# A transformer-layer kernel: one residual tile for all stages, and other places for splits and loads at its changes of stage

## Chip, core and metric

The kernel runs on one core of one Trainium2 chip. The metric is the device time of one launch in microseconds (us), as the median of several runs; less is better.

## What is computed

One decoder layer in float32, for 2048 tokens of width 1024. Cut to what matters here:

```
h = x
# 1. mixer: HGRN2 (4 heads, chunks of 64) beside sliding-window attention (8 heads of 64)
hn = rms_norm(h, norm1_g);  proj = hn @ w_in
h = h + concat(hgrn2(proj), window_attention(proj)) @ w_out
# 2. cross attention to 256 memory tokens, 4 heads of 128
h = h + cross_attention(rms_norm(h, norm2_g), rms_norm(mem, mem_norm_g)) @ xa_wo
# 3. MLP, 1024 -> 4096 -> 1024
a = relu(rms_norm(h, norm3_g) @ mlp_up);  h = h + (a * a) @ mlp_down
```

## The kernel before

All of it is one program in raw engine streams: TensorE (PE), VectorE (DVE), ScalarE (ACT), GpSimd (POOL) and SyncE (SP, the queue of nearly all loads and stores) each run a list written out by hand, and wait for one another on semaphores. The tokens are four blocks of 512, held transposed: a block is a tile of 128 partitions x 8 x 512. A weight panel is 128 x 1024 (512 KB). There are two slots for panels (`raw`, `whi`, `wlo`, index 0 and 1, taken in turn).

**Every product is made in three parts.** A float32 value is held as a high part (`hi`, `whi`: ACT's copy into fp32r) and a low part (`lo` by DVE, `wlo` by POOL: the value less its high part). A product of a panel with a block adds high x high, high x low and low x high: 24 matmuls of 512 columns for a panel of eight 128x128 pieces. So before PE can use a panel, it has been loaded by SP, split by ACT (`whi`, about 1 us) and by POOL (`wlo`, four pieces), and the slot that it goes into has been used up. `take` (ACT or DVE) empties the PSUM bank of a product; PE may start product n once product n-2 is taken.

**The stages**, in the order in which they run:

- `prepare` (L489 on): rope angles, normed memory, memory keys and values, and the norm of the first block. At its end SP stores the angles, the keys and the values to HBM (L566 to L571); the semaphore `kept` counts these three stores to 48.
- `mixer` (L745 on): first the list `FIRST_STEPS`, the products of five panels (numbers 17 to 21: hg_f, hg_q, hg_v, hg_g, sw_k) for the first block, with the gate work of its first head beside them; then four turns, one for each block, by `MIX_STEPS` (the last by `LAST_STEPS`, L238 to L251, made from `MIX_STEPS` by leaving out what prepares a next block). ACT begins with `act.wait_ge(sh["kept"], 48)` ahead of `FIRST_STEPS` (L1225). DVE waits for `kept` too, clears five buffers and sets one (L1278 to L1281), and only then starts its list. The mixed block goes from `yT` to HBM (`mixed_scratch`) in four stores.
- In the last turn, `cross_panel` splits the first panel of the next stage, and `cross_make` 0 to 2 puts its product among the steps of the last attention.
- `cross` (L1691 on): two turns, each for a pair of blocks, in the order `CROSS_WORK` (built at L267 to L333): the products `out` (8 panels for each block), `xq` (4), the attention, `xo` (4 panels with two products each). Products of `out` and `xo` are added to the residual `h` by DVE (L2011). At the end of turn 1 stand the products 32 to 39 (`xo` of the second block), and among them `norm_write`/`norm_store` (the first block of the pair, normed for the MLP, to HBM), `split` 0 to 7 (the high and low part of the first block of the MLP, L1911 and L1999) and `norm_square` 3 0 to 7 (squares of the other block, ACT L1940, summed by DVE L2021 to L2028).
- `mlp` (L2258 on): two halves of two blocks; up products with pairs of panels, the first pairs (`PLAIN`) plain and the others by Strassen's seven products, then 112 steps down. A plain pair makes four products, named by panel and block: "11", "12", "21", "22".

**SP at the change from mixer to cross** (L989 to L1003, L1819 to L1852). After the two stores of `yT`, SP waits for all four stores of the last block. Then it issues, in this order: memory keys and values (512 KB each), the residual block (2 MB, L1830), the second mixed block (2 MB, L1833), cross panel 2, and then each panel i once slot i - 2 is split (L1849 to L1851). The panels 0 and 1 were loaded in the last mixer turn. ACT splits panel 1 only when its mixer list is at its end: `split_panel` is the first step of `CROSS_WORK` (L1919).

**The change from cross to mlp.** SP loads MLP panel 0 into slot 0 as cross panel 32 (split by L1919 and L464), waits for the norm of the pair's first block (L1857), loads the second normed block into `h[:, 0]` (2 MB, L1858), and then MLP panel 1 (L1861). PE waits for the whole split of panel 0 and for all eight low parts of the block (`first_block_split`) before its first MLP product. ACT waits for the last product and the last sum of squares, and then runs `panel(0, 1)`, `moving` B12 and B22 (high parts of the second block), `plain` 11 (takes a product) and so on. DVE makes the low parts and the Strassen sums T1, T3, T2, T4. PE makes the products in the order 11, 12, 21, 22.

**Tiles.** `mixer` holds `yT`, `kq`, `key` and `keep` (the span factors of a head) as tiles of its own, `prepare` its `mT`, `msq`, `mn`; `h` (two blocks, 32 KB a partition) exists only from `cross` on.

Of the kernel before, what the change touches and what calls it, by code (L numbers as in the profile page):

```python
# [266 lines left out]
def cross_steps():  # L267
# [52 lines left out]
    for u in range(HEADS):  # L320
# [118 lines left out]
def layer(nc, xT, memT, pos, con_d, vec_d, sinks_d, w_mix, w_cross, w_mk, w_mv, w_mlp, outT):  # L439
# [6 lines left out]
    with ExitStack() as ctx:  # L446
        def sb(name, shape, dt=F32):
            return ctx.enter_context(nc.sbuf_tensor(name, shape, dt))

        sh = dict(con=sb("con", [P, CON_W]), vec=sb("vec", [P, VEC_W]), eps=sb("eps", [P, 1]), hT=sb("hT", [P, KT, TB]),  # L450
# [4 lines left out]
                  w_hi=ctx.enter_context(nc.semaphore("panel_hi_ready")),  # L455
                  cross_product=ctx.enter_context(nc.semaphore("c_product_ready")),
# [22 lines left out]
        with ExitStack() as inner:  # L479
# [3 lines left out]
            sh |= dict(h=sb("h", [P, 2, KT, TB]), aout=sb("aout", [P, 2, TB]), upper=inner.enter_context(ExitStack()))  # L483
# [5 lines left out]
def prepare(nc, block, sems, sh, memT, pos, con_d, vec_d, sinks_d, w_mk, w_mv, rope_d, mem_d, xT, w_mix):  # L489
# [9 lines left out]
    with ExitStack() as ctx:  # L499
# [13 lines left out]
        mT = sb("mT", [P, KT, MEM])  # L513
        msq = sb("msq", [P, KT, MEM])
        mn = sb("mn", [P, KT, MEM])
# [40 lines left out]
        def _(sp):  # L556
            sp.dma_start(mT[:], memT).then_inc(s_mem, 16)
# [187 lines left out]
def mixer(nc, block, sems, sh, xT, w_mix, rope_d, y_d, w_cross):  # L745
# [17 lines left out]
    with ExitStack() as ctx:  # L763
# [14 lines left out]
        yT = sb("yT", [P, KT, TB])  # L778
# [17 lines left out]
        key = sb("key", [P, TB])  # L796
        keep = sb("keep", [P, TB])
# [7 lines left out]
        kq = sb("kq", [P, NS, TB])  # L805
# [156 lines left out]
        def _(sp):  # L962
# [8 lines left out]
            def turn(blk, last):  # L971
# [20 lines left out]
                sp.dma_start(out[:, HEADS:KT - 1, :], yT[:, HEADS:KT - 1, :]).then_inc(stored[1].sem, 16)  # L992

# [35 lines left out]
        def _(act):  # L1029
# [80 lines left out]
            def turn(blk, steps):  # L1110
                for step in steps:
# [112 lines left out]

            act.wait_ge(sh["kept"], 48)  # L1225
            turn(-1, FIRST_STEPS[1:])
# [464 lines left out]
def cross(nc, block, sems, sh, xT, w_cross, mem_d, y_d, h2_d, normed_d, w_mlp):  # L1691
# [16 lines left out]
    with ExitStack() as ctx:  # L1708
# [34 lines left out]
        h_in = [signal(f"c_residual_loaded_{b}", 1, 16) for b in range(2)]  # L1743

        h_out = [signal(f"c_residual_stored_{b}", 1 + b, 16) for b in range(2)]
        raw_in = [signal(f"c_panel_loaded_{i}", CROSS_PAN // 2, 16) for i in range(2)]
        w_hi = signal("c_panel_hi_ready", CROSS_PAN)
# [68 lines left out]
        def _(sp):  # L1816
# [6 lines left out]
            for turn in range(TURNS):  # L1823
                last = turn == TURNS - 1
                for i in range(1, CROSS_PAN + 1):
                    if i == 1:
# [3 lines left out]
                        sp.dma_start(h[:, 0, :, :], xT[turn * 2]).then_inc(h_in[0].sem, 16)  # L1830
                    if i == 2:
# [16 lines left out]
                    if (turn, i) != (0, 1):  # L1848
# [30 lines left out]
        def _(act):  # L1879
# [33 lines left out]
            for turn, step in CROSS_WORK:  # L1913
                kind = step[0]
                if kind == "split_panel":
# [4 lines left out]
                elif kind == "take" and CROSS_PRODUCTS[step[1]][1] == "xq":  # L1920
# [11 lines left out]
                    act.activation(hsq[:, u % 2, :], PROJ[n % 2][:], ACT.Square).then_inc(q_in.sem, 1)  # L1932
                elif kind == "split":
# [255 lines left out]

def product_order(half):  # L2190


    for n in range(PAIRS):
        yield from ((n, j) for j in (OUTPUTS if n < PLAIN[half] else ("P1", "P2", "P5", "P6", "P3", "P7", "P4")))
# [63 lines left out]
def mlp(nc, block, sems, sh, w_mlp, h2_d, normed_d, hidden_d, outT):  # L2258
# [8 lines left out]
    with ExitStack() as ctx:  # L2267
# [3 lines left out]
        def sem(name):  # L2271
            return sems.enter_context(nc.semaphore(name))
# [128 lines left out]
        w_hi = Tally(sem("m_weight_hi_ready"), w_keys + steps)  # L2401
# [858 lines left out]
```

## Time and profile before

| | us |
|---|---|
| median of 3 runs | 2741.36 (2741.07 to 2743.33) |
| the profiled execution: its own time | 2745.06 |
| its span in the trace | 2743.3 |
| PE busy | 2643.8 (96%) |
| DVE / ACT / POOL busy | 1771.7 / 1146.9 / 1073.5 |

The span is what the trace covers, from the first to the last instruction; the execution's own time is 1.8 us longer. Times in the rows further down are from the span's start, the mean duration of one instruction in ns. PEclk is the clock that was granted to TensorE, as a share of 2.4 GHz: 1.00, or 0.50 for 1.2 GHz. A matmul that follows another starts before that one's end, so the rate of a stretch is read from starts, not from durations. By these times `prepare` ends at about 53, `mixer` at about 1019 and `cross` at about 1499 us.

### The profile page before, as it was taken

The numbers are of one execution on the slowest core, as the hardware profiler recorded it, in microseconds if no ns is written. First come the engines' busy times: TensorE is split into PE (matmuls) and PEld (weight loads), VectorE is DVE, ScalarE is ACT, GpSimd is POOL, SyncE is SP. The second block draws the span as 40 slices with busy tenths as digits, with TensorE's granted clock in tenths as the row PEclk, the third lists the DMA queues.
The fourth block names the chain that finished last, engine by engine and source line by source line (L and its number), as shares of the span: only waits on it lengthen the run. The fifth ranks groups of instructions, "written<-read, shape, count | busy, mean of one in ns | idle before, by whom it ended". The sixth has DMA issues, their size and how long they took to land.

```text
span 2743.3 us, 39704 instructions
## 1 busy us (share of the span) xinstructions
PE 2643.8 (96%) x13654; PEld 2165.0 (79%) x13654; DVE 1771.7 (65%) x3010; ACT 1146.9 (42%) x2179; POOL 1073.5 (39%) x1258
## 2 busy tenths in 40 slices
PE   7999999999999988998998999999999999999999
PEld 5778778777877876786886788878888888888887
DVE  6677567767756754656657587687666354556665
ACT  4455454545544443554465432243223223322332
POOL 1332322233232215525634477647667222222223
PEclk9999999999999989999999999999999999999999
DMA  4211311221131114317314234433334963445664
GB/s 177 95 49 46 110 55 47 69 96 54 40 118 54 45 67 174 107 54 285 130 49 170 85 131 140 160 104 112 123 109 138 314 188 112 134 134 144 202 186 149
DMA packets 172701, 326.17 MB, mean 119 GB/s; under 512 B 11856, under 2 KB 77776, under 8 KB 169808
## 3 DMA queue, kind: packets, MB, share of 16 engines
q1 hardware_dynamic: 167344, 314.08, 34.3%
q10 hardware_dynamic: 5152, 9.51, 0.9%
q8 instruction: 110, 1.80, 0.3%
q14 instruction: 95, 0.78, 0.1%
HBM read 255.26 MB, written 68.29 MB: 118 GB/s over the span
## 4 chain that ended last, share of the span: by engine, by line
PE 80%; DVE 9%; ACT 5%; issue 3%; DMA 2%; POOL 1%; ACTq 0%; DVEq 0%; SPq 0%; POOLq 0%
PE bank L3176 7%; PE bank L3174 7%; PE bank L3178 7%; PE bank L3154 7%; PE bank L3150 6%; PE bank L3151 6%; PE bank L1520 5%; PE bank L1513 5%; PE bank L1516 5%; PE bank L1592 3%; PE bank L2123 3%; PE bank L2118 3%; PE bank L2119 3%; PE bank L1675 2%; PE bank L1652 2%
## 5 line engine op out<-in xcount | busy, mean ns | idle before, releaser
L464 POOL TENSOR_TENSOR wlo<-raw,whi 128x256 fp32r<-128x256 f32 x612 | 506.5, 858 | 992.3 <-ACT whi L1117 648.2
L1513 PE MATMUL bank<-hi,whi 128*128 128x512 f32 x704 | 296.3, 421 | 5.3 <-ACT whi L1117 5.3
L1516 PE MATMUL bank<-lo,whi 128*128 128x512 f32 x704 | 278.8, 396 | 5.9 <-DVE lo L1267 5.9
L3178 PE MATMUL bank<-hi,wlo 128*128 128x512 f32 x896 | 275.8, 389 | 0.0
L3174 PE MATMUL bank<-hi,whi 128*128 128x512 f32 x896 | 275.8, 389 | 0.0
L3176 PE MATMUL bank<-lo,whi 128*128 128x512 f32 x896 | 275.8, 389 | 0.0
L2675 POOL TENSOR_TENSOR wlo<-h,whi 128x256 fp32r<-128x256 f32 x160 | 127.9, 823 | 300.1 <-ACT whi L2736 300.1
L2981 DVE TENSOR_TENSOR lo<-h,hi 128x1024 fp32r<-128x1024 f32 x80 | 124.5, 1557 | 172.8 <-ACT hi L2744 172.8
L2118 PE MATMUL bank<-hi,whi 128*128 128x512 f32 x504 | 210.3, 417 | 24.4 <-ACT whi L1919 17.2
L2119 PE MATMUL bank<-lo,whi 128*128 128x512 f32 x504 | 199.5, 396 | 0.0
L2657 POOL TENSOR_TENSOR wlo<-raw,whi 128x256 fp32r<-128x256 f32 x166 | 150.1, 930 | 121.2 <-ACT whi L2685 118.9
L3178 PEld LDWEIGHTS bank<-hi,wlo 128*128 128x128 f32 x896 | 168.2, 188 | 34.9
L3174 PEld LDWEIGHTS bank<-hi,whi 128*128 128x128 f32 x896 | 168.2, 188 | 34.9
L3176 PEld LDWEIGHTS bank<-lo,whi 128*128 128x128 f32 x896 | 168.2, 188 | 34.9
L1520 PE MATMUL bank<-hi,wlo 128*128 128x512 f32 x704 | 190.3, 412 | 0.0
L2736 ACT ACTIVATE whi<-h 128x512 fp32r<-128x512 f32 x80 | 50.6, 632 | 289.1 <-PE bank L3178 271.3
L1516 PEld LDWEIGHTS bank<-lo,whi 128*128 128x128 f32 x704 | 134.1, 190 | 38.1 <-DVE lo L1267 8.5
L1513 PEld LDWEIGHTS bank<-hi,whi 128*128 128x128 f32 x704 | 134.0, 190 | 37.8 <-issue 10.5
L2657 POOL TENSOR_TENSOR m_xlo<-raw,m_xhi 128x256 fp32r<-128x256 f32 x174 | 162.7, 967 | 0.0
L1520 PEld LDWEIGHTS bank<-hi,wlo 128*128 128x128 f32 x704 | 130.6, 189 | 35.2 <-issue 9.2
L2685 ACT ACTIVATE whi<-raw 128x512 fp32r<-128x512 f32 x87 | 54.5, 629 | 225.0 <-DMA raw<-w_mlp 181.9
L3150 PE MATMUL bank<-hi,whi 128*128 128x512 f32 x348 | 136.1, 391 | 1.7 <-issue 1.7
(387 smaller groups left out, 5981.9 us busy)
## 6 DMA issues: line engine op xcount, KB each, us to landing
h<-hidden_scratch SPq DMA_DIRECT2D x96, 512.0 KB, 4.2
raw<-w_mix SPq DMA_DIRECT2D x88, 512.0 KB, 3.3
raw<-w_cross SPq DMA_DIRECT2D x64, 512.0 KB, 3.3
raw<-w_mlp SPq DMA_DIRECT2D x64, 512.0 KB, 4.7
hidden_scratch<-hT SPq DMA_DIRECT2D x116, 256.0 KB, 2.1
h<-w_mlp SPq DMA_DIRECT2D x112, 256.0 KB, 3.0
hT<-xT SPq DMA_DIRECT2D x4, 2048.0 KB, 9.4
hT<-mixed_scratch SPq DMA_DIRECT2D x4, 2048.0 KB, 8.6
```

Source lines behind the costliest of these rows:

```text
L464: last = pool.tensor_tensor(wlo[:, i, cols], raw[:, i, cols], whi[:, i, cols].bitcast(F32), ALU.subtract)
L1513: pe.matmul(out, w, hi[:, k, :], start=k == 0, stop=False)
L1516: pe.matmul(out, w, lo[:, k, :], start=False, stop=False)
L1520: last = pe.matmul(out, wlo[:, i % 2, k * P:(k + 1) * P], hi[:, k, :], start=False, stop=k == KT - 1)
L2118: pe.matmul(out, w, hi[b][:, k, :], start=k == 0, stop=False)
L2119: pe.matmul(out, w, lo[b][:, k, :], start=False, stop=False)
L2657: last = pool.tensor_tensor(lo_tile[:, cols], source(half, n, w)[:, cols], hi_tile[:, cols].bitcast(F32), ALU.subtract)
L3150: pe.matmul(acc, hi_tile[:, cols], parts(half, m, k)[0], start=k == 0, stop=False)
L3154: last = pe.matmul(acc, lo_tile[:, k * P:(k + 1) * P], parts(half, m, k)[0], start=False, stop=k == KH - 1)
L3174: pe.matmul(down_bank(i)[:], wh[:, cols], xh[:, i % 2, :], start=K == 0, stop=False)
L3176: pe.matmul(down_bank(i)[:], wh[:, cols], xl[:, i % 2, :], start=False, stop=False)
L3178: last = pe.matmul(down_bank(i)[:], wl[:, cols], xh[:, i % 2, :], start=False, stop=K == KD - 1)
```

## The change

It touches the three changes of stage, and what has to hold for that.

- **One tile.** `h` is made once for all stages. `yT` is its second half. `kq`, `key` and `keep` of the mixer lie in its first half, and so do (with four pieces of the second half) `mT`, `msq` and `mn` of `prepare`.
- **prepare to mixer.** ACT does the steps of `FIRST_STEPS` ahead of the first `take` (that is, the split of panel 18) before it waits for `kept`.
- **mixer to cross.** In the last turn SP loads cross panel 2 once panel 0 is split, and the residual block once the last head's scores are made, both ahead of its wait for the last stores. ACT splits cross panel 1 in the last attention (`cross_second`, ahead of `("pv", 12)`). In `cross`, SP no longer loads these, and issues the second mixed block ahead of panel 4, not of panel 2.
- **cross to mlp.** `norm_square` 3 4 to 3 7 move behind all splits; ahead of them ACT splits MLP panel 1 (`mlp_panel`). SP loads MLP panel 1 before the second normed block. PE waits for the high parts alone before its first MLP product, makes high x high and low x high first, and waits for the low parts one by one (`first_plain`). The first pair's order becomes 11, 21, 12, 22, on PE and in the takes and stores; ACT's list at the start of the MLP changes with it.

```diff
@@ LAST_STEPS, CROSS_WORK
-                      (("cross_make", 1), ("scores", _first + 3)), (("cross_make", 2), ("pv", _first))):
+                      (("cross_make", 1), ("scores", _first + 3)), (("cross_make", 2), ("pv", _first)), (("cross_second",), ("pv", _first))):
...
+def last_squares_end(work):
+    end = SEQ // TB // 2 - 1
+    late = [(end, ("norm_square", 3, k)) for k in range(KT // 2, KT)]
+    return [s for s in work if s not in late] + [(end, ("mlp_panel",))] + late
...
+CROSS_WORK = last_squares_end(CROSS_WORK)
@@ prepare, mixer: tiles
-        mT = sb("mT", [P, KT, MEM])
...
+        places = sh["h"][:].rearrange("p i k t -> p (i k) t")
+        mT, msq, mn = (places[:, n * KT // 2:(n + 1) * KT // 2, :].rearrange("p k (a t) -> p (k a) t", t=MEM) for n in range(3))
...
-        yT = sb("yT", [P, KT, TB])
+        residual, yT = sh["h"][:, 0], sh["h"][:, 1]
+        kq, key, keep = residual[:, 0:NS, :], residual[:, NS, :], residual[:, NS + 1, :]
@@ mixer, SP, end of turn
+                if last:
+                    sp.wait_ge(set_up, COUNTS_SET)
+                    wait_all(sp, sh["split_for_cross"])
+                    sp.dma_start(raw[:, 0, :], w_cross[CROSS_SOURCE[2]]).then_inc(sh["cross_raw_in"], 16)
+                    sp.wait_ge(h_sc.sem, h_sc.at(blk, HEADS * NCH // 2 - 1))
+                    sp.dma_start(residual, xT[0]).then_inc(sh["residual_in"], 16)
@@ mixer, ACT
+                    elif kind == "cross_second":
+                        act.wait_ge(set_up, COUNTS_SET)
+                        act.wait_ge(*sh["loaded_for_cross"])
+                        act.activation(whi[:, 1, :], raw[:, 1, :], ACT.Copy).then_inc(sh["cross_hi"], 1)
...
+            first_take = next(n for n, s in enumerate(FIRST_STEPS) if s[0] == "take")
+            turn(-1, FIRST_STEPS[1:first_take])
             act.wait_ge(sh["kept"], 48)
-            turn(-1, FIRST_STEPS[1:])
+            turn(-1, FIRST_STEPS[first_take:])
@@ cross, SP
-                        sp.dma_start(h[:, 0, :, :], xT[turn * 2]).then_inc(h_in[0].sem, 16)
-                    if i == 2:
+                        if turn:
+                            sp.dma_start(h[:, 0, :, :], xT[turn * 2]).then_inc(h_in[0].sem, 16)
+                    if i == (2 if turn else 4):
                         sp.wait_ge(y_lo.sem, y_lo.at(turn, KT - 1))
                         sp.dma_start(y[:], y_d[turn * 2 + 1]).then_inc(y_in[1].sem, 16)
...
-                    if (turn, i) != (0, 1):
+                    if turn or i > 2:
...
+            sp.wait_ge(w_hi.sem, w_hi.at(TURNS - 1, CROSS_PAN - 1))
+            sp.wait_ge(w_lo.sem, w_lo.at(TURNS - 1, CROSS_PAN - 1))
+            sp.dma_start(raw[:, 1, :], w_mlp[1]).then_inc(sh["panel_in"], 16)
             sp.wait_ge(h_out[0].sem, h_out[0].at(TURNS - 1, 0))
             sp.wait_ge(n_w[0].sem, n_w[0].at(TURNS - 1, KT - 1))
             sp.dma_start(h[:, 0, :, :], normed_d[1].rearrange("k p t -> p k t")).then_inc(sh["second_in"], 16)
-            sp.wait_ge(w_hi.sem, w_hi.at(TURNS - 1, CROSS_PAN - 1))
-            sp.wait_ge(w_lo.sem, w_lo.at(TURNS - 1, CROSS_PAN - 1))
-            sp.dma_start(raw[:, 1, :], w_mlp[1]).then_inc(sh["panel_in"], 16)
@@ cross, ACT
-                if kind == "split_panel":
+                if kind == "split_panel" and (turn, step[1]) == (0, 1):
+                    continue
+                elif kind == "split_panel":
...
+                elif kind == "mlp_panel":
+                    act.wait_ge(sh["panel_in"], 16)
+                    act.wait_ge(product.sem, product.at(turn, len(CROSS_PRODUCTS) - 1))
+                    act.activation(whi[:, 1, :], raw[:, 1, :], ACT.Copy).then_inc(sh["mlp_hi"], 1)
@@ mlp, order, ACT, PE
+def plain_order(half, n):
+    return ("11", "21", "12", "22") if (half, n) == (0, 0) else OUTPUTS
...
-            wait_all(act, sh["last_products"] + sh["squares_added"] + sh["norms_stored"])
+            wait_all(act, sh["squares_added"] + sh["norms_stored"])
...
-                    panel(0, 1)
                     moving(0, "B12")
+                    plain(0, 0, "11")
                     moving(0, "B22")
-                    plain(0, 0, "11")
                     moving(0, "T1")
+                    plain(0, 0, "21")
                     plain(0, 0, "12")
+                    panel(0, 2)
                     moving(0, "T2")
-                    plain(0, 0, "21")
-                    panel(0, 2)
                     moving(0, "T4")
...
+            def first_plain(acc):
+                for k in range(KT):
+                    pe.matmul(acc, whi[:, 0, k * P:(k + 1) * P], sh["hi"][:, k, :], start=k == 0, stop=False)
+                for k in range(KT):
+                    pe.matmul(acc, wlo[:, 0, k * P:(k + 1) * P], sh["hi"][:, k, :], start=False, stop=False)
+                y_lo, count = sh["first_block_split"][1]
+                for k in range(KT):
+                    pe.wait_ge(y_lo, count - (KT - 1) + k)
+                    last = pe.matmul(acc, whi[:, 0, k * P:(k + 1) * P], sh["lo"][:, k, :], start=False, stop=k == KT - 1)
+                last.then_inc(made.sem, 1)
...
-            wait_all(pe, sh["first_panel_split"] + sh["first_block_split"])
+            wait_all(pe, sh["first_panel_split"] + sh["first_block_split"][:1])
```

## Rows read from the trace of the kernel before

**Rows 1.** Page, part 4: the chain that ended last, shares of the span.
```profile
PE 80%; DVE 9%; ACT 5%; issue 3%; DMA 2%; POOL 1%; ACTq 0%; DVEq 0%; SPq 0%; POOLq 0%
```
**Rows 2.** Waits of PE: line, releaser: us in total, times, longest.
```profile
PE bank L2118 <- ACT whi L1919: 17.2, 3, 11.5
...
PE bank L3129 <- DVE lo L1999: 5.6, 1, 5.6
PE bank L1513 <- ACT whi L1117: 5.3, 1, 5.3
...
PE bank L3134 <- POOL wlo L2665: 1.4, 1, 1.4
```
**Rows 3.** Timeline, prepare to mixer: start, us, engine, line, operation [idle before <- releaser].
```profile
51.34 1.98 PE L1520 MATMUL bank<-hi,wlo 128*128 128x512 f32 x8
...
57.41 1.06 ACT L1117 ACTIVATE whi<-raw 128x1024 fp32r<-128x1024 f32 x1 [6.04 <-DMA memory_scratch<-memv]
...
63.03 0.66 DVE L1293 TENSOR_SCALAR fg<-fg 128x512 f32<-128x512 f32 x1
...
68.45 0.53 DVE L1316 TENSOR_TENSOR kq<-hq,fg 128x256 f32<-128x256 f32 x1 [0.85 <-ACT hq L1087]
...
79.18 0.97 DVE L1359 TENSOR_TENSOR qdec<-kq,span 128x256 f32<-128x256 f32 x1
...
83.31 0.60 PE L1567 MATMUL bank<-con,kend 128*128 128x128 f32 x4
```
**Rows 4.** Busy time by window; last columns: PEclk, DMA share, GB/s.
```profile
58.60:63.60 5.00, 4.99 (x12) 3.98 (x13) 4.69 (x6) 1.35 (x2) 5.00 (x8) 0.50 0.23 58
...
1012.00:1018.60 6.60, 5.59 (x43) 4.31 (x41) 2.69 (x13) 2.95 (x8) 0.00 (x0) 1.00 0.00 0
...
1018.60:1021.80 3.20, 0.06 (x2) 0.06 (x1) 0.00 (x0) 1.65 (x2) 0.10 (x1) 1.00 0.45 169
```
**Rows 5.** Timeline of SP's queue, mixer to cross and cross to mlp.
```profile
1022.96 0.43 SPq L1822 DMA_DIRECT2D c_memv<-memory_scratch  x1
...
1023.91 0.42 SPq L1833 DMA_DIRECT2D hT<-mixed_scratch  x1
...
1491.18 0.38 SPq L1858 DMA_DIRECT2D h<-normed_scratch  x1
1494.13 0.33 SPq L1861 DMA_DIRECT2D raw<-w_mlp  x1
```
**Rows 6.** DMA issues in 1022.5:1025 (last column: us to landing).
```profile
hT<-mixed_scratch SPq DMA_DIRECT2D x1, 2048.0 KB, 14.2
...
c_memv<-memory_scratch SPq DMA_DIRECT2D x1, 512.0 KB, 5.1
raw<-w_cross SPq DMA_DIRECT2D x1, 512.0 KB, 14.9
```
**Rows 7.** Timeline, mixer to cross, as group 3.
```profile
1015.29 0.60 ACT L1211 ACTIVATE pT<-bank 128x512 f32<-128x512 f32 x1 [0.81 <-PE bank L1663]
...
1024.43 22.04 SPq L1851 DMA_DIRECT2D raw<-w_cross  x4
...
1047.45 0.39 PE L2118 MATMUL bank<-hi,whi 128*128 128x512 f32 x1
...
1052.89 0.39 PE L2118 MATMUL bank<-hi,whi 128*128 128x512 f32 x1
```
**Rows 8.** DMA issues in 1491:1492.
```profile
h<-normed_scratch SPq DMA_DIRECT2D x1, 2048.0 KB, 9.7
```
**Rows 9.** Timeline, cross to mlp, as group 3.
```profile
1495.07 4.22 POOL L464 TENSOR_TENSOR wlo<-raw,whi 128x256 fp32r<-128x256 f32 x4 [1.02 <-ACT whi L1919]
...
1502.96 0.68 DVE L2011 TENSOR_TENSOR h<-bank,h 128x512 f32<-128x512 f32 x1
...
1504.53 0.77 PE L3129 MATMUL bank<-hi,whi 128*128 128x512 f32 x1 [5.63 <-DVE lo L1999]
...
1511.51 0.39 PE L3129 MATMUL bank<-m_thi,whi 128*128 128x512 f32 x1
```

More of the change, by code:

```diff
@@ L448, in sb @@
             return ctx.enter_context(nc.sbuf_tensor(name, shape, dt))
[L450 removed]
+        sh = dict(con=sb("con", [P, CON_W]), vec=sb("vec", [P, VEC_W]), eps=sb("eps", [P, 1]), hT=sb("hT", [P, KT, TB]), h=sb("h", [P, 2, KT, TB]),
                   hi=sb("hi", [P, KT, TB], F32R), lo=sb("lo", [P, KT, TB], F32R), raw=sb("raw", [P, 2, KT * P]),
@@ L455, in layer @@
                   w_hi=ctx.enter_context(nc.semaphore("panel_hi_ready")),
+                  residual_in=ctx.enter_context(nc.semaphore("c_residual_loaded_0")),
+                  cross_raw_in=ctx.enter_context(nc.semaphore("c_panel_loaded_0")),
+                  cross_hi=ctx.enter_context(nc.semaphore("c_panel_hi_ready")),
+                  mlp_hi=ctx.enter_context(nc.semaphore("m_weight_hi_ready")),
                   cross_product=ctx.enter_context(nc.semaphore("c_product_ready")),
@@ L481, in sb @@
                 return inner.enter_context(nc.sbuf_tensor(name, shape, dt))
-            sh |= dict(h=sb("h", [P, 2, KT, TB]), aout=sb("aout", [P, 2, TB]), upper=inner.enter_context(ExitStack()))
+            sh |= dict(aout=sb("aout", [P, 2, TB]), upper=inner.enter_context(ExitStack()))
             sh |= {n: sh["upper"].enter_context(nc.sbuf_tensor(n, [P, KT, TB], F32R)) for n in ("hi1", "lo1")}
@@ L556, in _ @@
         def _(sp):
-            sp.dma_start(mT[:], memT).then_inc(s_mem, 16)
+            sp.dma_start(mT, memT).then_inc(s_mem, 16)
             sp.dma_start(con[:], con_d).then_inc(s_con, 16)
@@ L795, in mixer @@
         w2 = sb("w2", [P, TB])
-        key = sb("key", [P, TB])
-        keep = sb("keep", [P, TB])
         span = sb("span", [P, TB])
@@ L1742, in cross @@
         y_in = [signal(f"mixed_loaded_{b}", 1, 16) for b in range(2)]
-        h_in = [signal(f"c_residual_loaded_{b}", 1, 16) for b in range(2)]
+        h_in = [Signal(sh["residual_in"], 1, 16), signal("c_residual_loaded_1", 1, 16)]
+        signals.append(h_in[0])
         h_out = [signal(f"c_residual_stored_{b}", 1 + b, 16) for b in range(2)]
-        raw_in = [signal(f"c_panel_loaded_{i}", CROSS_PAN // 2, 16) for i in range(2)]
-        w_hi = signal("c_panel_hi_ready", CROSS_PAN)
+        raw_in = [Signal(sh["cross_raw_in"], CROSS_PAN // 2, 16), signal("c_panel_loaded_1", CROSS_PAN // 2, 16)]
+        signals.append(raw_in[0])
+        w_hi = Signal(sh["cross_hi"], CROSS_PAN, 1)
+        signals.append(w_hi)
         w_lo = signal("c_panel_lo_ready", CROSS_PAN)
@@ L2187 @@
 OUTPUTS = ("11", "12", "21", "22")
+def plain_order(half, n):
+    return ("11", "21", "12", "22") if (half, n) == (0, 0) else OUTPUTS
 def product_order(half):
     for n in range(PAIRS):
-        yield from ((n, j) for j in (OUTPUTS if n < PLAIN[half] else ("P1", "P2", "P5", "P6", "P3", "P7", "P4")))
+        yield from ((n, j) for j in (plain_order(half, n) if n < PLAIN[half] else ("P1", "P2", "P5", "P6", "P3", "P7", "P4")))
 WEIGHT_ORDER = ("A11", "A12", "S1", "S2", "S4", "S3", "A22")
@@ L2400, in mlp @@
             w_keys += [(half, n, w) for n in range(PLAIN[half], PAIRS) for w in WEIGHT_ORDER]
-        w_hi = Tally(sem("m_weight_hi_ready"), w_keys + steps)
+        w_hi = Tally(sh["mlp_hi"], w_keys + steps)
         w_lo = Tally(sem("m_weight_lo_ready"), w_keys + steps)
@@ L2412, in mlp @@
         for half in HALVES:
-            taken_keys += [(half, n, e + o) for n in range(PLAIN[half]) for o in OUTPUTS for e in "rq"]
+            taken_keys += [(half, n, e + o) for n in range(PLAIN[half]) for o in plain_order(half, n) for e in "rq"]
             for n in range(PLAIN[half], PAIRS):
@@ L2600, in _ @@
                             load_tile(half + (n + 1) // PAIRS, (n + 1) % PAIRS, j)
-                    for o in ("11", "12", "21", "22") if n < PLAIN[half] else ("11", "12", "22", "21"):
+                    for o in plain_order(half, n) if n < PLAIN[half] else ("11", "12", "22", "21"):
                         if (half, n, o) != (0, 0, "11"):
@@ L3123, in plain @@
                 names = ("B12", "B22") if b else ("B11", "B21")
+                if (half, p) == (0, 0) and not b:
+                    first_plain(acc)
+                    return
                 for k in range(KT):
@@ L3182, in down @@
                     last.then_inc(made.sem, 1)
-            wait_all(pe, sh["first_panel_split"] + sh["first_block_split"])
+            wait_all(pe, sh["first_panel_split"] + sh["first_block_split"][:1])
             for half, n, j in whole_order:
-                if (half, n) == (0, 0) and OUTPUTS.index(j) < 2:
-                    wait_all(pe, sh["residual_updated"][OUTPUTS.index(j):][:1])
+                if (half, n) == (0, 0) and j in ("11", "21"):
+                    wait_all(pe, sh["residual_updated"][j == "21":][:1])
                 if (half, n, j) == (0, 3, "P1"):
```

3 lines of the change are left out of this document (removed).

## The prediction

> **What bounds the kernel now.** First the chain that ended last: TensorE holds 80% of it, and DMA only 2% [rows 1]. So time is to be had where PE stands still or runs at its lower clock. Then PE's waits over the whole span: nearly all are under 2 us, and the large ones are single events at the three changes of stage [rows 2]. One of 5.3 us ends the first panels' work, one of 11.5 us stands inside the 17.2 us of L2118, one of 5.6 us is the first MLP product. These are the places that the change touches. Third, the pitch: in a steady stretch one product of 24 matmuls starts 5.44 us after the last (1047.45 to 1052.89) [rows 7]. All terms below are differences of starts, so a clock that has dropped is inside them. That it drops is seen behind the 5.3 us wait: 58.6 to 63.6 at PEclk 0.50, which is 1.2 GHz, only 12 matmuls in 5 us [rows 4].
>
> **Prepare to mixer.** ACT stood 6.04 us for the store of the memory values before it split panel 18, at 57.41; PE had ended panel 17 at 53.3 (51.34 + 1.98) [rows 3]. After the change the split runs at about 51.4, PE goes straight on, and panel 18 is made from 53.3 to 58.8 at full clock. What is late next? The first `take` still waits for `kept`, to 57.4 (0.6 us); the split of panel 19 comes behind it, at 58 to 59 or later by its load, so panel 19 starts at 59.3 to 60.1 and ends by 65.5. Panel 20 needs `take` 18, which stands behind the gate work; that needs DVE's L1293 at 63.03, and DVE's start is not touched by the change (it waits for `kept` and clears its buffers). ACT's two gate steps of 0.63 us end at 65.0, the split of 20 at 66.1, `take` 18 at 66.7. Panel 20 from 66.8, 21 from 72.2, ended at 77.7. Then PE needs `kend` and `qdec` for the transposes of L1567, at 83.31 before. DVE's chain to them ran from 68.45, where it had lost 0.85 us to ACT's hq, to 80.15 (79.18 + 0.97) [rows 3]. It comes 0.85 us earlier, 79.3, so PE passes at 79.4. **Term A: 83.31 - 79.4 = 3.9 us.** The idle time and the slow clock were worth 5.3 + 12 x 0.2 = 7.7; the rest goes into waits for ACT and DVE. Bounds: 1.5 if the three short waits let the clock drop once more (2.4 us), 5.3 if that DVE chain runs faster.
>
> **Mixer to cross.** Four steps.
> - `cross_second` puts a 1.06 us copy between ACT's copies for scores 13 and 14. ACT stood idle 0.81 there, up to 1015.29 [rows 7], so 0.25 us is on the path and pushes the last `pv` from 1018.6 to 1018.9. Its sum, DVE and PE steps are else untouched.
> - Product 1 then starts at 1019.0: both parts of panel 1 are there (POOL needs 2.8 us from 1015.5).
> - Panel 2 was loaded near 990, when its slot was split; the residual block follows near 993. SP has nothing else between 979 and 1022.6, and the DMA share of 1012 to 1018.6 is 0.00 [rows 4], so both cost nothing; without that cover the 2 MB would cost 5 us in the queue (below). ACT splits panel 2 at 1020.9 to 1021.9, POOL to 1024.8; product 2 starts at 1024.4 and needs the low part at 1028.
> - SP still waits for the last stores, so memory keys and values go out as before (values issued 1022.96, landed 5.1 later, 1028.1) [rows 5, 6]. Right behind comes panel 3. The queue's steady rate is seen at the second mixed block and panel 2: issued 1023.91 and 1024.43, landed 14.2 and 14.9 us later, 1038.1 and 1039.3 [rows 5, 6, 7]; so 1.2 us for 512 KB, and two 2 MB blocks in 10.0, 5.0 each. Panel 3 lands at 1029.5, is split at 1030.55, and product 3 starts at 1030.7, 0.9 late. The mixed block (now ahead of panel 4) lands at 1034.5, panel 4 at 1035.8, split at 1036.9: product 4 starts at 1037.05, 0.9 late. Panels 5 and 6 have no block before them; the second residual block ahead of panel 7 was there before.
>
> Before, product 4 started at 1052.89 [rows 7]. **Term B: 15.8 us.** Bounds: 17.6 with no wait at all (1019.0 + 3 x 5.44 = 1035.3); 10.7 if the block still lands 14.2 us after its issue (1038.3; product 4 at 1040.7, 12.2) and the clock drops once behind that wait (1.5).
>
> Here the trace and a page differ. PEclk is 1.00 through the last attention, 1012 to 1018.6, though transposes stand among its matmuls, and still 1.00 in the idle 3.2 us behind it [rows 4]; so I take product 1 at full clock. The Trainium skill (TensorE: Matmul & The Clock Gate, "Part 4: PE-mode transpose") says that transposes do not count as busy time for the clock; by that product 1 could start at 1.2 GHz although PE never stopped, some 1.5 us less gain, inside B's bounds.
>
> **Cross to mlp.** PE ended product 39 near 1498.9 and stood 5.63 us, to 1504.53 [rows 9]. Its releaser was the last low part; DVE made it behind the residual sums (the last `take` at 1502.96) and sums of squares, each of which waited for ACT's square. With four squares moved back, ACT's splits run on (0.55 us each behind panel 32's, 1494.3 to 1497.8) and DVE has `take` 39 at 1499.0 and the last low part at 1500.3. POOL ended MLP panel 0 at 1499.3 (1495.07 + 4.22) and comes 0.6 earlier, as ACT is. So all that the first product waits for is there at 1498.7: it starts at 1498.95, no low part is asked for before 1502.6, and the clock has no idle time to drop in. Before, this product took 6.98 us (1504.53 to 1511.51); now 5.44.
> - Panel 1: SP issues it at 1494.15 as before (its wait is for the slot), but now ahead of the block; it lands at 1497.6 (about 3.4 us for a lone 512 KB). ACT splits it once product 39 is made, 1499.0 to 1500.0, POOL to 1504.2. "21" needs it at 1504.4 and 1508. Hidden.
> - The second block is issued 3.3 us later (1491.18 becomes 1494.5) [rows 5] and took 9.7 [rows 8]: 1504.2. The squares end at 1503.4. B12 is split by ACT 1504.2 to 1506.4 and low by 1507.2. "12", now third, asks for it at 1509.8: hidden by "21", 2.6 us of slack. In the old order it would be asked for at 1504.4 and cost 1.5 and more.
> - Takes, B22, T1 to T4 keep their chain on DVE, 2.4 us earlier than before, and are wanted only at the third pair. SP's stores change order only.
> - Panel 2 of the MLP can be split once "12" is made (1515.3), behind its take: whi at 1517.7. POOL took 7.0 us for it beside DVE's sums: low x high was due at 1531.5, and PE waited 1.4 [rows 2]. Again 7.0 gives 1524.7, against a need at 1524.3: 0.4 stays.
>
> **Term C: 5.6 idle + 1.5 clock + 1.0 of that wait = 8.1 us.** Bounds 4.5 (the second block or B12 3 us later than taken, plus a slow POOL) and 8.6.
>
> **Sum: 3.9 + 15.8 + 8.1 = 27.8 us.** The new places of `yT`, `kq`, `key`, `keep`, `mT` change no instruction, and no row shows a cost by place: nothing (0 to 2 us either way). Against the profiled execution of 2745.06 us that is 2717.3. The median of 3 runs is 3.7 lower, and the gain is of single events, the same in each run: 2741.36 - 27.8 = 2713.6.
>
> **Rivals.**
> - **Late loads.** The 2 MB in front of panel 4, or the values in front of panel 3, hold PE as before: B is 10.7. For it: L2118 <- ACT whi is DMA time, and SP's start at 1022.6 has not moved. Against: 2 MB less stand in the queue. Sum 22.7: 2718.7. Chance 0.17.
> - **The MLP wait only moves.** "12" or panel 2 waits instead: C is 4.5, sum 24.2: 2717.2. Against: 2.6 us of slack. Chance 0.08.
> - **All covered.** 5.3 + 17.6 + 8.6 = 31.5: 2709.9. Chance 0.08.
> - **It doesn't do what it says.** The early places are held up by waits that stand there already (`kept`, the stores, the slots): 2741.4. Against: each releaser named above is gone from the list in question. Chance 0.02.
> - **Slower: the clock.** The change breaks three long stops into short ones around products. If the clock then stays at 1.2 GHz in the products between them, each takes 10.2 us (24 x 0.425, the pitch of the slow stretch) in place of 5.44, 4.8 more. With four products at each place, 57 us are lost, 2741.4 - 27.8 + 57 = 2771. It decides from six products on (27.8 / 4.8). Against: the slow stretch read follows a stop of 5.3 us and is over 5 us later [rows 2, 4], and none is left that long. The Trainium skill (TensorE: Matmul & The Clock Gate, "HAM oscillation — how this bites in real kernels") tells of a kernel that drops again at each wait for a load; no trace here shows it for waits of 1 us. Chance 0.02.
>
> Forecast: 0.63.
>
> **The numbers.** About 0.2% (5.5 us) is what a measurement of this kernel can tell from no change. All cases but the last two are faster by over 20 us: faster 0.96, same 0.02, slower 0.02. The range takes in late loads and the MLP case with 2 us for the places, and "all covered": 2709 to 2721.
>
> **What would show it.** L1513 no longer waits 5.3 us; L1567's first start is near 79.4. PE's first `cross` matmul follows the last `pv` at once; product 4 starts 15 to 16 us earlier relative to the last attention; two waits L2118 <- ACT whi of about 1 us stand in the place of 11.5. No wait of over 0.5 us ahead of the first MLP product, none ahead of "12", PEclk 1.00 behind it. Wrong if one of those new waits is over 3 us, if a window of 0.50 stands behind one of the three places, or if `mixer` between its ends takes another time than before.

## The result: 16.8 us faster, less than forecast

| | before | after |
|---|---|---|
| median, us | 2741.46 (2741.07 to 2743.33, 4 runs) | 2724.70 (2721.09 to 2725.99, 4 runs) |
| profiled execution / span | 2745.06 / 2743.3 | 2723.78 / 2722.0 |

The ratio is 0.9935 (95%: 0.9922 to 0.9948). The forecast was 2713.6 with a range of 2709 to 2721, so the median lies outside by 3.7 us, on the slow side. The two profiled executions differ by 21.3 us and the medians by 16.8; where these 4.5 us are is told with the experiment `before_again`.

Waits of PE in the kernel after (columns as in [rows 2]), over the whole span:

```profile
PE bank L3184 <- POOL wlo L2701: 7.5, 1, 7.5
...
PE bank L2149 <- DVE h L2042: 5.8, 4, 1.9
```

The waits of 11.5, 5.6 and 5.3 us of [rows 2] are gone. One wait of 7.5 us is new: L3184 is the low x high part of a plain MLP product, and POOL's L2701 makes its low part. The one of 1.4 us for POOL in [rows 2] stood at the same line; it has grown by 6.1.

**Prepare to mixer.** PE's waits in 50 to 84 us, and its timeline at the transposes of `kend`:

```profile
PE bank L1534 <- ACT whi L1132: 1.9, 1, 1.9
PE bank L1588 <- ACT qdec L1167: 1.8, 1, 1.8
```
```profile
81.62 0.63 PE L1588 MATMUL bank<-con,kend 128*128 128x128 f32 x4 [1.83 <-ACT qdec L1167]
```

The transposes start at 81.62, before at 83.31 [rows 3]: 1.7 us gained of the 3.9 forecast. PE now arrives early and waits for ACT's `qdec`, which waits for DVE. The landing of the last store (`kept`) differs between executions. Counted from DVE's first clearing, right behind it, the transposes start at 25.8 us before (83.31 less 57.55) and at 23.2 after (81.62 less 58.46), so 2.6 us are the change's and 0.9 were lost to the landing.

Behind the wait of 1.9 us the clock fell for some microseconds, as the window shows:

```profile
58.00:64.00 6.00, 4.12 (x13) 3.00 (x12) 4.75 (x7) 1.65 (x2) 2.81 (x4) 0.79 0.34 128
```

PE still came to the transposes 1.8 us too early for `qdec`, so this fall cost nothing there.

**Mixer to cross.** The timeline of PE: first matmul of product 1, then of the products 3 and 4. The second fence shows two windows: their length, busy time and count of PE, PEld, DVE, ACT and POOL, and as in [rows 4] PEclk, DMA share and GB/s.

```profile
1013.64 0.50 PE L2149 MATMUL bank<-hi,whi 128*128 128x512 f32 x1
...
1025.06 0.47 PE L2149 MATMUL bank<-hi,whi 128*128 128x512 f32 x1 [0.23 <-ACT whi L1946]
...
1031.22 0.47 PE L2149 MATMUL bank<-hi,whi 128*128 128x512 f32 x1 [0.44 <-ACT whi L1946]
```
```profile
1008.00:1013.60 5.60, 4.80 (x40) 3.95 (x39) 2.40 (x9) 3.59 (x9) 2.78 (x4) 1.00 0.00 1
1013.60:1031.00 17.40, 16.96 (x74) 13.36 (x72) 1.56 (x3) 3.70 (x4) 5.65 (x8) 1.00 0.79 299
```

Product 1 follows the last attention without a gap, and the clock is 1.00 on both sides. From there to product 4 it is 17.6 us. Before, PE was done with the mixer at 1018.6 (product 1 started at 1021.77 after 3.14 of idle time) and product 4 started at 1052.89 [rows 7], 34.3 later. So this place gives 16.7 us; 15.8 were forecast.

**Cross to mlp.** Timeline of PE, in order: the first MLP product, the second product, the 7.5 us wait, and the first of Strassen's products.

```profile
1477.43 2.06 PE L3154 MATMUL bank<-hi,whi 128*128 128x512 f32 x8 [0.20 <-DVE h L2042]
...
1482.96 0.39 PE L3179 MATMUL bank<-hi,whi 128*128 128x512 f32 x1
...
1510.57 1.65 PE L3184 MATMUL bank<-hi,wlo 128*128 128x512 f32 x3 [7.50 <-POOL wlo L2701]
...
1531.17 0.39 PE L3200 MATMUL bank<-hi,whi 128*128 128x512 f32 x1
```

The windows around that wait:

```profile
1500.00:1508.00 8.00, 3.07 (x14) 2.22 (x12) 7.88 (x14) 5.59 (x10) 8.00 (x1) 0.83 0.00 0
1508.00:1520.00 12.00, 9.43 (x31) 7.62 (x32) 0.00 (x0) 1.46 (x3) 5.26 (x8) 0.68 0.38 132
```

The first product starts 0.2 us after PE is free and lasts 5.5, as forecast. Then PE stands from 1503.1 to 1510.6, and behind that the granted clock of twelve microseconds is 0.68, so part of it ran at 1.2 GHz. The first Strassen product of the kernel before starts in this row:

```profile
1551.27 0.39 PE L3150 MATMUL bank<-hi,whi 128*128 128x512 f32 x1
```

Before, PE was free at 1498.9 (1504.53 less 5.63 [rows 9]) and came to it 52.4 us later. After, it was free at 1477.2 and took 53.9. **The third part, forecast at 8.1 us, cost 1.6 us by this landmark.** The sum of the three places is 1.7 + 16.7 - 1.6 = 16.8 us, which is also the difference of the medians.

### The profile page after: what moved, and what is told of

The parts are those of the page before. It is cut to its first block, busy times and chain, and to the rows that moved or that the text cites. A ratio compares the mean times of both kernels' runs of the same rounds, so it can differ in the third digit from the quotient of the medians.

```text
span 2722.0 us, 39706 instructions
## 1 busy us (share of the span) xinstructions
PE 2639.5 (97%) x13654; PEld 2163.4 (79%) x13654; DVE 1767.9 (65%) x3010; ACT 1147.2 (42%) x2179; POOL 1082.8 (40%) x1258
## 4 chain that ended last, share of the span: by engine, by line
PE 78%; DVE 9%; ACT 5%; issue 4%; DMA 2%; POOL 2%; ACTq 0%; DVEq 0%; SPq 0%; POOLq 0%
PE bank L3224 7%; PE bank L3226 7%; PE bank L3228 7%; PE bank L3204 6%; PE bank L3200 6%; PE bank L3201 6%; PE bank L1541 5%; PE bank L1534 5%; PE bank L1537 5%; PE bank L1613 3%; PE bank L2154 3%; PE bank L2149 3%; PE bank L2150 2%; PE bank L1696 2%; PE bank L1673 2%
```

## What POOL did meanwhile

POOL's and DVE's timelines in the kernel after, from 1493 on. POOL makes the low parts of MLP panels 2 and 3 (eight pieces); DVE makes the second block's low parts (L2883) and Strassen's sums (L2900), four instructions a row.

```profile
1497.43 15.82 POOL L2701 TENSOR_TENSOR wlo<-raw,whi 128x256 fp32r<-128x256 f32 x8 [14.78 <-ACT whi L2727]
```
```profile
1495.76 2.49 DVE L2883 TENSOR_TENSOR lo<-hT,hi 128x512 fp32r<-128x512 f32 x4
...
1505.40 2.48 DVE L2883 TENSOR_TENSOR m_tlo<-hT,m_thi 128x512 fp32r<-128x512 f32 x4
```

And POOL's timeline again, cut at 1499, where only what began before is counted:

```profile
1497.43 11.03 POOL L2701 TENSOR_TENSOR wlo<-raw,whi 128x256 fp32r<-128x256 f32 x1 [14.78 <-ACT whi L2727]
```

One piece of panel 2 took 11.03 us. It ended at 1508.46, 0.6 us after DVE's last instruction (1507.88), and the other seven, of both panels, were done 4.8 us later. In the kernel before it was the same, later in the chain and so shorter; POOL cut at 1530, and DVE's last row:

```profile
1525.90 4.98 POOL L2665 TENSOR_TENSOR wlo<-raw,whi 128x256 fp32r<-128x256 f32 x1 [15.44 <-ACT whi L2691]
```
```profile
1527.80 2.48 DVE L2848 TENSOR_TENSOR m_tlo<-hT,m_thi 128x512 fp32r<-128x512 f32 x4
```

1530.88 against 1530.28: again 0.6 us behind. So most of the 7.0 us that the forecast took for POOL's work was no duration of that work. It was a wait for the end of DVE's chain.

This holds where DVE's run is under way when POOL begins. In the kernel before, POOL had begun on panel 1 half a microsecond ahead of DVE's first four low parts, and there the two took turns, 1.2 us a piece (POOL's and DVE's timelines):

```profile
1506.28 4.18 POOL L2665 TENSOR_TENSOR wlo<-raw,whi 128x256 fp32r<-128x256 f32 x4 [6.98 <-ACT whi L2691]
```
```profile
1506.76 4.26 DVE L2848 TENSOR_TENSOR m_tlo<-h,m_thi 128x512 fp32r<-128x512 f32 x4 [1.69 <-ACT m_thi L2716]
```

There it was DVE that paid, with 4.26 us for what took 2.50 without POOL (the row of 1485.30, in the part on why the prediction was wrong).

## Experiments

The theories that the expectations number: that the third part gives nothing, since one chain, by DVE to POOL's low part of panel 2, ends equally late with and without it (theory 1); that the loss of part C is POOL's, which gets nowhere while DVE's sums run without a gap (theory 2); that the later landing of the second block holds up DVE's chain (theory 3); that in part A DVE's list from `kept` on sets the transposes, with the clearing of `kpad` in it (theory 4).

### Without part C

`no_c` is the change without its third part: `last_squares_end`, `mlp_panel`, `first_plain`, `plain_order` and the new order on SP and ACT are left out.

```diff
-CROSS_WORK = last_squares_end(CROSS_WORK)
...
-            sp.dma_start(raw[:, 1, :], w_mlp[1]).then_inc(sh["panel_in"], 16)
             sp.wait_ge(h_out[0].sem, h_out[0].at(TURNS - 1, 0))
...
+            sp.dma_start(raw[:, 1, :], w_mlp[1]).then_inc(sh["panel_in"], 16)
```

> The change without its third part (cross to mlp as before). Theory 1, the third part gives nothing: the chain of the second block, through the Strassen sums on DVE to the low part of MLP panel 2 on POOL, ends 33 to 34 us behind product 39 in both kernels. Then this kernel takes as long as the whole change, 2723 to 2726 us, and from the last cross product to the first Strassen product it takes 52.8 us as in the kernel before (54.3 in the changed one). Rival, the third part gives the 8 us of the prediction and something elsewhere takes them: 2732 to 2734 us.

Measured: 2724.98 us (2721.40 to 2726.36, 5 runs), ratio 0.9936 (0.9922 to 0.9950); after: 2724.70 and 0.9935. The third part brings nothing that these runs can tell. PE's timeline shows the old wait back at its place; the one for POOL's low part behind it is 0.3 us:

```profile
1481.98 0.77 PE L3148 MATMUL bank<-hi,whi 128*128 128x512 f32 x1 [5.61 <-DVE lo L2018]
```

POOL was done with panel 2 34.1 us after PE was free (1510.44 less 1476.37), against 33.3 with the change (1510.51 less 1477.23): theory 1 stands. One wait and one slow stretch were exchanged for another of about the same price.

### DVE waits for POOL

`w_t2` and `w_t4` are the change with one wait more on DVE, ahead of the sum T2 or of the later T4:

```diff
+                if half == 0:
+                    dve.wait_ge(w_lo.sem, w_lo.upto(0, 2, "panel"))
                 moving_sum(half, "T2")
```

> The changed kernel, with one wait more: DVE waits for the low part of MLP panel 2 before it makes the sums T2. Theory 2, POOL gets nowhere while DVE runs one operation right behind the other: DVE's stop lets POOL make the four pieces in some 3 us, PE's wait of 7.5 us goes to under 0.5 and with it the low clock behind it; first Strassen product 43.5 to 45 us behind the last cross product in place of 54.3, about 10 us less in all, 2713 to 2717 us. Rival, POOL itself needs 13 us for this panel (or its input comes late): PE's wait stays at 7 us or more, the pieces stay over 2 us each, and the time stays at 2724 or gets longer by what DVE loses.

> The same wait, one stage later, before DVE makes the sums T4. Theory 2: DVE gets there 5.6 us after POOL has begun, and POOL is done 2.7 us later, so PE waits about 2.8 us in place of 7.5: some 5 to 6 us less than the changed kernel. Rival: the wait stays at 7 us.

Measured for T2: 2715.73 us (2711.28 to 2718.25, 4 runs), ratio 0.9898 (0.9883 to 0.9913), 9.0 below the change. For T4: 2719.07 in one execution. POOL's and DVE's timelines with the wait ahead of T2:

```profile
1500.51 3.50 POOL L2701 TENSOR_TENSOR wlo<-raw,whi 128x256 fp32r<-128x256 f32 x4 [14.74 <-ACT whi L2727]
...
1504.05 2.50 DVE L2900 TENSOR_TENSOR h<-h,hT 128x512 f32<-128x512 f32 x4 [2.72 <-POOL wlo L2701]
```

DVE stopped at 1501.33; POOL's first piece ended 0.6 us later, the other three took 0.7 us each, and DVE lost 2.72 us that it could spare. No wait of PE over 0.7 us is left here, and the clock stays up (windows of `w_t2`):

```profile
1500.00:1508.00 8.00, 8.00 (x37) 6.64 (x36) 5.28 (x10) 2.88 (x5) 3.50 (x4) 1.00 0.10 36
1508.00:1520.00 12.00, 11.27 (x51) 8.98 (x50) 7.06 (x12) 7.89 (x13) 2.83 (x4) 1.00 0.36 104
```

With the wait ahead of T4, PE's wait for POOL is 2.1 us (2.8 expected). POOL's timeline, cut at 1503, and DVE's:

```profile
1497.34 6.24 POOL L2701 TENSOR_TENSOR wlo<-raw,whi 128x256 fp32r<-128x256 f32 x1 [14.16 <-ACT whi L2727]
```
```profile
1500.50 2.49 DVE L2883 TENSOR_TENSOR m_tlo<-h,m_thi 128x512 fp32r<-128x512 f32 x4
1505.66 2.49 DVE L2900 TENSOR_TENSOR hT<-hT,h 128x512 f32<-128x512 f32 x4 [2.67 <-POOL wlo L2701]
```

The first piece now ends at 1503.58, 0.6 us after DVE's last instruction at 1502.99. The piece's length follows from where DVE's run ends: 11.03 us in the change, 6.24 here, 4.98 in the kernel before. That is theory 2, and for this chain it stands. An instruction added to an engine with work to spare gave what the whole third part was meant to give: from where PE is free to the first Strassen product it is 44.8 us (1480.35 to 1525.20, by the two rows below, `w_t2` again) against 53.9 with the change and 52.4 before, so 7.5 of the 8.1 us forecast.

```profile
1480.53 0.47 PE L3156 MATMUL bank<-hi,whi 128*128 128x512 f32 x1 [0.18 <-DVE h L2042]
...
1525.20 0.39 PE L3202 MATMUL bank<-hi,whi 128*128 128x512 f32 x1
```

### The second block first

`block_first` is the change with SP's two loads in the old order, the 2 MB block ahead of MLP panel 1.

```diff
-            sp.dma_start(raw[:, 1, :], w_mlp[1]).then_inc(sh["panel_in"], 16)
...
             sp.dma_start(h[:, 0, :, :], normed_d[1].rearrange("k p t -> p k t")).then_inc(sh["second_in"], 16)
+            sp.dma_start(raw[:, 1, :], w_mlp[1]).then_inc(sh["panel_in"], 16)
```

> The changed kernel, with SP's loads in the old order: second normed block first, then MLP panel 1. Theory 3, the chain on DVE starts when this block has landed (7.8 us behind the last cross product): with the old order it starts 3 to 4 us earlier and PE's wait for the low part of panel 2 falls from 7.5 to about 4; but panel 1 now comes late and POOL's pieces of it fall beside DVE's work, so a new wait of some us stands in product 21. Sum: between 3 us less and 3 us more. Rival, the landing of the block does not matter: DVE's first low part of B12 starts as before, and only the new wait is added.

Measured: 2725.05 us in one execution, no better than the change. Theory 3 had DVE's chain start earlier with the block. ACT's and DVE's timelines show why it didn't:

```profile
1481.82 1.06 ACT L1963 ACTIVATE whi<-raw 128x1024 fp32r<-128x1024 f32 x1 [4.81 <-DMA raw<-w_mlp]
```
```profile
1483.43 3.11 DVE L2059 TENSOR_TENSOR c_sqsum<-c_sqsum,c_sq 128x512 f32<-128x512 f32 x3 [2.79 <-ACT c_sq L1971]
...
1488.38 2.50 DVE L2883 TENSOR_TENSOR m_tlo<-h,m_thi 128x512 fp32r<-128x512 f32 x4 [0.70 <-ACT m_thi L2752]
```

ACT waits 4.81 us for the panel behind the block; the squares stand behind that split, the sums of squares behind them, and DVE begins B12 at 1488.38, 10.2 us after PE was free at 1478.2, against 8.1 us with the change (1485.30 less 1477.2). The wait for POOL is 7.8 us. The edit moved two things at once, so it doesn't test theory 3 alone: the late panel, which ACT splits ahead of the squares, hides what an earlier block would give. The change's own trace bounds that: ACT stood idle 1.85 us for the block. This run holds one more instance of theory 2 (POOL's timeline cut at 1503):

```profile
1500.51 11.04 POOL L2701 TENSOR_TENSOR wlo<-raw,whi 128x256 fp32r<-128x256 f32 x1 [13.37 <-ACT whi L2727]
```

### Part A alone

`a_only` is the kernel before with the new places of the tiles and `turn(-1, FIRST_STEPS[1:first_take])` ahead of the wait for `kept`.

> The kernel before with the tiles of the change (yT, kq, key, keep, mT in the one tile h) and its first part (split of panel 18 before the wait for kept) alone. By the trace of the changed kernel the transposes of kend come at 81 to 82 us (83.3 before) and the time is 1.5 to 2.5 us less than before; by the prediction 79.4 and 3.9 less. If the new places of the tiles cost or save something, the four turns of the mixer (transposes of kend, turn 0 to turn 3) take other than the 717.2 to 718.4 us of the traces so far.

Measured: 2739.30 us (2736.94 to 2740.71, 11 runs) beside 2741.56 (2738.73 to 2743.89, 15 runs); the ratio 0.9993 (0.9984 to 1.0002) can't be told from 1. By PE's timeline the transposes start where they do in the change:

```profile
81.64 0.41 PE L1570 MATMUL bank<-con,kend 128*128 128x128 f32 x2 [1.65 <-ACT qdec L1149]
```

So the first part is worth about 2 us by the trace (2.6 counted from `kept`, as in the change), and the tiles' new places cost nothing that a run shows.

### The clearing of kpad moved to POOL

`both` is the change with the wait of `w_t2`, and with the largest of DVE's five clearings on POOL, behind the split of panel 18:

```diff
-            for t in (state[:], kpad[:], vsw[:, QT, :], vtok[:], rope[:, 1, :]):
+            for t in (state[:], vsw[:, QT, :], vtok[:], rope[:, 1, :]):
...
+                        if isinstance(blk, int) and (blk, i) == (-1, AHEAD + 1):
+                            pool.wait_ge(sh["kept"], 48)
+                            pool.memset(kpad[:], 0.0).then_inc(set_up, 1)
```

> The changed kernel with DVE's wait before T2 (as in the run w_t2) and, besides, the largest of the six buffer clears at the start of the mixer (kpad, 2.19 us) moved from DVE to POOL, behind POOL's part of panel 18. Theory 4: the first term of the prediction came out at 1.7 in place of 3.9 us because DVE's list from the landing of the last store (kept) to kend and qdec sets the end; so 2.2 us less on DVE before the first gate step bring PE to the transposes of kend at 79 to 79.6 in place of 81.6, and the time to 2711 to 2714. Rival: ACT or PE itself sets it, the transposes stay at 81 to 82 and the time is that of w_t2, 2715.7.

Measured: 2710.59 us (2708.89 to 2714.81, 4 runs), ratio 0.9894 (0.9879 to 0.9909). By its median it is the fastest kernel here, 31 us below the kernel before and 14 below the change. Its ratio can't be told from that of `w_t2` (0.9898), so what the move of `kpad` gives is read from the trace, not from the times. The timelines of POOL and PE:

```profile
57.50 2.23 POOL L1036 MEMSET kpad<- 128x2560 f32 x1 [2.35 <-DMA memory_scratch<-memv]
```
```profile
78.90 0.63 PE L1591 MATMUL bank<-con,kend 128*128 128x128 f32 x4 [1.44 <-ACT qdec L1170]
```

The transposes start 2.7 us earlier than in the change. `kept` came 0.85 earlier in this execution, so 1.9 are the edit's, and DVE had spent 2.19 us on `kpad` (shown further down). Theory 4 stands: DVE's list behind `kept` sets the end of this stage.

### The residual block loaded late

`residual_late` is the change with the 2 MB load of the residual back in `cross`, ahead of panel 3.

```diff
-                    sp.wait_ge(h_sc.sem, h_sc.at(blk, HEADS * NCH // 2 - 1))
-                    sp.dma_start(residual, xT[0]).then_inc(sh["residual_in"], 16)
...
-                        if turn:
+                        if True:
```

> The changed kernel, with the load of the residual block (2 MB) back in the next stage, behind memory keys and values and now ahead of panel 3. Theory of the prediction, the loads share one queue at 2.4 us per MB: panel 3 and panel 4 land 5 us later, product 4 starts 22.5 to 23 us behind the last pv in place of 17.8, and 1 to 2 us more if the clock falls. Rival, the gain came from the early panels 1 and 2 alone: 17.8 stays.

Measured: 2734.29 us in one execution, 10.5 above the profiled execution of the change (2723.78). Product 4 starts at 1042.86, 28.6 us after product 1 (1014.23) in place of 17.6. The loss of 11 is twice what the queue's 5.0 us for 2 MB would give. PE's and DVE's timelines show another way than the queue:

```profile
1029.83 0.79 PE L2147 MATMUL bank<-hi,whi 128*128 128x512 f32 x1 [9.85 <-DVE h L2040]
```
```profile
1029.09 1.29 DVE L2040 TENSOR_TENSOR h<-bank,h 128x512 f32<-128x512 f32 x2 [18.18 <-issue]
```

The first products of `cross` are added to the residual, so DVE can empty no bank before it is there. It was issued at 1018.96 and landed 9.7 us later; both banks were full, and PE stood 9.85 us. The kernel before had the same chain, covered by its wait for panel 2 (11.47 us). Without the load ahead of time this place gives 5.7 us (34.3 less 28.6) of its 16.7.

### The kernel before, once more

> The kernel before once more, for a second trace. Its profiled execution was 3.7 us above the median. If that sits in the mixer (turn 3's transposes of kend to the last pv: 217.5 us in the first trace, 214.5 to 217.5 in the changed kernels), this one takes 214.5 to 217 there, at a clock of 0.50 for a shorter time; the stretches at the changes of stage repeat within 0.5 us (34.5 from the last pv to product 4, 52.8 from the last cross product to the first Strassen product).

Measured: 2745.05 us, its profiled execution, 3.5 above the median of 15 runs beside it. The windows 990 to 1000, in the mixer's last turn, first of `before_again`, then of `a_only`, then of the change:

```profile
990.00:1000.00 10.00, 10.00 (x57) 8.73 (x56) 7.90 (x17) 0.00 (x0) 0.99 (x2) 0.50 0.00 0
```
```profile
990.00:1000.00 10.00, 10.00 (x66) 8.59 (x65) 7.99 (x20) 1.75 (x6) 0.00 (x0) 0.82 0.00 0
```
```profile
990.00:1000.00 10.00, 10.00 (x66) 8.55 (x65) 7.89 (x21) 1.91 (x7) 0.00 (x0) 0.83 0.66 262
```

Both profiled executions of the kernel before have PEclk 0.50 here. It isn't the change that mends this: `a_only` has 0.82 without parts B and C, and `w_t2` has 0.50 with them. From the last transposes of `kend` to the last `pv` it is 40.8 us in both executions of the kernel before and in `w_t2`, 37.1 in `a_only` and in the change. So it differs between executions; over the four turns of the mixer it makes some 3 of the 4.5 us by which the two profiled ones differ more than the medians. Where the rest is isn't shown. The waits at the changes of stage repeat: 5.4, 5.6 and 1.4 us for the 5.3, 5.6 and 1.4 of [rows 2].

## Why the prediction was wrong

- **What bounds the kernel** was read rightly: PE's single waits at three changes of stage. The second behaved as the chain of waits said, the first gave under half, and the third gave nothing.
- **Term B (15.8 forecast, 16.7 measured).** The order held: product 1 at once and at full clock, panel 2 in time, two waits for `whi`. They are 0.23 and 0.44 us in place of 0.9 each. The loads went as forecast (5.2 us for the values, 5.0 more for the mixed block), but SP issued the values 3.6 us after the last `pv` (1017.32 less 1013.71), where the forecast had 4.1 (1022.96 less 1018.9): panel 3 was split at 1023.86, panel 4 at 1030.02. The rule on transposes from "Part 4: PE-mode transpose" of the Trainium skill's page TensorE: Matmul & The Clock Gate would have product 1 slow; the windows show 1.00 behind an attention with transposes, so it didn't bear on this place.
- **Term A (3.9 forecast, 1.7 measured).** The failed step is "It comes 0.85 us earlier, 79.3". DVE's last step before the transposes (`qdec`) started at 81.05. It was 79.18 before [rows 3], and the forecast had it 0.85 us earlier still. `kept` came 0.9 us later in this execution, and the operations between took longer: from 68 to 84 us twelve of them take over 0.7 us, before eight. They do so beside POOL. Of the two copies below (DVE's timeline, after) the one inside POOL's second row takes 0.82 us and the one in the gap behind it 0.28. Since PE and the splits come earlier, POOL's third panel is made at 75.17, inside the chain; before, it was made at 78.83, at the chain's end. The forecast moved the chain's start and left out that its pace depends on POOL. That this is POOL's doing is read from the rows; no run takes POOL's work away from there. The clearing of `kpad` ahead of it takes 2.19 us.

```profile
59.43 2.19 DVE L1301 MEMSET kpad<- 128x2560 f32 x1 [0.48 <-ACT fg L1099]
...
71.89 0.82 DVE L1361 COPY h<-h 128x256 f32<-128x256 f32 x1
...
74.60 0.28 DVE L1361 COPY h<-h 128x256 f32<-128x256 f32 x1
```

POOL's timeline beside it, after:

```profile
70.81 3.38 POOL L476 TENSOR_TENSOR wlo<-raw,whi 128x256 fp32r<-128x256 f32 x4 [0.34 <-ACT whi L1132]
75.17 3.09 POOL L476 TENSOR_TENSOR wlo<-raw,whi 128x256 fp32r<-128x256 f32 x4 [0.98 <-ACT whi L1132]
```

And before:

```profile
78.83 3.30 POOL L464 TENSOR_TENSOR wlo<-raw,whi 128x256 fp32r<-128x256 f32 x4 [2.11 <-ACT whi L1117]
```

- **Term C (8.1 forecast, -1.6 measured).** This is the error that put the time outside the range. The steps up to the first product held (0.2 us of wait, 5.5 for the product, "12" without a wait). The failed step is "POOL took 7.0 us for it beside DVE's sums ... Again 7.0 gives 1524.7". A duration was carried over that was an end: POOL is done about 2.7 us after DVE's chain, whenever it starts. And that chain hardly moved against the end of `cross`: it starts when B12 is split, 8.1 us after PE is free (the row below, of DVE's timeline in the change), 7.9 before (1506.76 less 1498.9). The gain took PE some 7 us closer to it, and PE ran into it. Asked in this way, the rows of before give it: POOL was done at 1532.9, 34.0 us after PE was free, and PE wanted the low part 1.4 us ahead of that [rows 2], at 32.6. Less 5.6 and 1.5 us that is 25.5, so PE would wait some 8.5 us, and 7.5 were measured; the clock falls behind it.

```profile
1485.30 2.50 DVE L2883 TENSOR_TENSOR m_tlo<-h,m_thi 128x512 fp32r<-128x512 f32 x4 [1.32 <-ACT m_thi L2752]
```

- **The second block** landed 11.4 us after its issue, not 9.7, with panel 1 ahead of it; of that the chain got 1.85 us of idle time on ACT. Small, and `block_first` shows that the old order is no better.
- **The rival "The MLP wait only moves"** was the right one, with chance 0.08. It named panel 2, but priced it at 3.6 us; it took all of C and 1.6 more. "Late loads" didn't come. The clock fell behind two of the three places, which the forecast named as a sign of being wrong, but for a few microseconds each (0.79 in 58 to 64, 0.68 in 1508 to 1520) and not for product after product, as the slow rival had it. It doesn't fall at the first place each time: in `both`, behind a wait of 2.0 us there, PEclk of 60 to 70 is 1.00.
- **From profile to median.** The forecast took the gain from single events and subtracted it from the median. That held: the three measured terms are 16.8 us, as is the difference of the medians. That they agree to a tenth is luck, since the ratio's interval allows 14 to 21 us, and by `kept` alone the first term shifts by 0.9.

## What to carry to other kernels

A duration read beside another engine's busy stretch may be that engine's end in disguise: compare the ends before carrying the duration to another place. Where one engine's unbroken run holds up another's work, a short wait on the one with time to spare can be worth more than moving work: here one wait gave 9 us. Before a wait is removed, ask what the engine will reach next and when that will be ready, counted from the same event; and a load that only an accumulation needs still holds PE, as soon as both banks are full.

## What the chip showed that was not expected

- DVE too is slower beside POOL: a 128x256 copy takes 0.82 us in place of 0.28.
- POOL's `tensor_tensor` (two inputs in SBUF, 128x256) got nowhere while a run of DVE's `tensor_tensor` (128x512) that was already under way went on without a gap: one piece took 11.03, 11.04, 6.24 and 4.98 us and ended 0.6 us after DVE's run in all four, against 0.7 us a piece with DVE still (seven in 4.8 us). The Trainium skill says in GPSIMD Engine Reference, section "1. Specifications", that POOL shares its SBUF interfaces with DVE when DVE has two SBUF inputs; the traces agree. Its page SBUF — State Buffer ("SBUF: two separate sides") calls it an exclusive lock for one instruction, which whoever starts first gets; here POOL did not get in between DVE's instructions of 0.68 us, for some 17 of them in the longest case (10.3 us at one each 0.60). But where POOL's pieces had begun first (1506.28 in the kernel before), the two engines took turns, and beside DVE's shorter operations at 70.81 and 75.17 us POOL got in and it was DVE that slowed down. What decides between these cases is not shown.
- A 2 MB load took 7.9 us (the residual, 0.4 us behind a panel of 512 KB, nothing else moving) and 11.4 us (the second normed block, also 0.4 us behind a panel, while stores ran beside it). What makes the difference was not tested.
- The granted clock of a stretch of the mixer's last turn differs between executions of the same kernel (0.50 or about 0.82 in the same 10 us), by some 3 us of time.
